# Transformer block pair in fp32 on one core: where the memory squares, the first low parts and the first down panels' high parts stand in the queues of a feed-forward stage

## The chip, the cores and the metric

One Trainium2 chip, one core of it. The metric is the device time of one execution in microseconds (us); of several runs the median is given. Engines are named as in the profile: PE is TensorE, DVE VectorE, ACT ScalarE, POOL GpSimd, SP SyncE, which issues the weight loads.

## What is computed

A sequence of 512 tokens of width 1024 goes through two blocks. The first is a feed-forward (2816 wide), a mixer, an attention over 256 memory tokens and a second feed-forward; the second block is a mixer of three branches and a third feed-forward. What matters here is cut to this:

```python
def swiglu(h, w1, w3, w2):
    return (jax.nn.silu(h @ w1) * (h @ w3)) @ w2

def first_block(x, mem, ...):
    x = x + 0.5 * swiglu(rms_norm(x, norm_ffn1[l]), ffn1_w1[l], ffn1_w3[l], ffn1_w2[l])
...
    x = x + memory_attention(rms_norm(x, norm_mem_q[l]), rms_norm(mem, norm_mem_kv[l]), ...)
    x = x + 0.5 * swiglu(rms_norm(x, norm_ffn2[l]), ffn2_w1[l], ffn2_w3[l], ffn2_w2[l])

def second_block(x, mem, ...):
...
    x = x + rmsnorm((jax.nn.silu(gate) * up) @ w_ffn_down[l], g_post_ffn[l])
```

All inputs are float32. `rms_norm(mem)` needs the mean square of the memory over its 1024 features, 8 tiles of 128.

## The kernel before

All activations lie feature-first in SBUF: `x` is 8 tiles of 128 features by 512 tokens, `hid` 22 tiles for the hidden layer, `memh` 8 tiles by 256 memory tokens. Each float32 product is made of three fp32r products: a high part of both operands, high by low and low by high. ACT copies a weight panel to its high part (`parts[..][0]`, semaphore `highs`), POOL subtracts to get the low part (`splits`), and PE may then use the panel. For activations ACT makes the high part (`hhis`) and DVE the low part (`hlos`).

**A feed-forward stage** runs three times (`ffn`, `ffn_up`, `ffn_down` on each engine). It begins with eight whole panels (two of them before the norm is known), whose products make the hidden tiles 0 to 3. Then come 9 pairs of hidden tiles (`PAIRS` = 8 turns of a loop and a last turn written out), each pair done by a seven-product scheme of blocks with sums and differences of quarter panels. PE runs `pair(0)`, `pair(1)` in each turn, 14 quarter products of 12 matmuls; the last turn has 12 quarter products. DVE makes three sums of weights for each half turn (`weight_sum_1`, `_2`, `_4`, in PSUM banks 3 and 7), the low parts of these sums (`sum_low`, `vlows`), and the gate and hidden tiles (`gate_first`, `up_second`, `gate_second`, `gate_scaled`, `pair_hidden`). ACT makes the high parts (`step_high`), copies partial outputs (`second_sum`, `third_taken`, `seed`) and does the silu (`pair_silu`). POOL makes four low parts (`first_lows`) and a difference for each half turn. Each engine goes through its own list in order, and the lists meet in semaphores; in a loop their values are computed from the turn.

**The down projection** takes 32 panels of 4 or 7 k-tiles (`CHUNKS`), eight banks at a time. Its first chunk uses the hidden tiles 0 to 3, whose high and low parts lie in `stores[0]` (tensor `bigr`). On ACT `high_part` makes a panel's high part; it waits for the panel's load and for the product that frees the parts.

In the first and second feed-forward DVE also sums the squares of the memory: `memory_square(k)` is a multiply into `sc` and an add into `ssum`, each waiting for the one before (`msteps`). PE turns the sum into column sums by `memory_norm` (L915), ahead of the first down panel, and waits there for `msums`. The third feed-forward has no memory squares (`loads` is None).

Where that work stands before: square 0 ahead of the pairs; squares 1 to 4 at the end of turns 0 to 3, square 5 behind turn 3 and 6 behind turn 7, between two loops; square 7 behind the last turn, in front of `memory_norm`. `EARLY` cuts the 8 turns in two loops of 4, and behind each loop two tiles of high parts (ACT, L2428) and low parts (DVE, `low_part`, L3182) of the first chunk are made. ACT makes the high parts of the down panels 0 and 1 behind the last `pair_silu` (L2457, L2458).

## Time and profile before

| | us |
|---|---|
| median of 3 runs | 2347.22 (2346.03 to 2347.31) |
| profiled execution, its own time | 2360.01 |
| span from first to last instruction | 2358.2 |
| PE busy in the span | 2262.5 (96%) |
| DVE, ACT, POOL busy | 1108.2, 1070.6, 1153.8 (47%, 45%, 49%) |

The mean granted clock of PE is 0.983 of full speed. A timeline row gives start, length, engine, line, what it writes and reads, and in brackets how long the engine was idle before it and what ended that. Matmul lengths overlap; starts are what to subtract.

### The profile page before, as it was taken

The page shows a single profiled execution, that of the slowest core. Times are in us where ns is not written, and L with a number is a line of the kernel's source. Part 1 is how long each engine was busy: PE and PEld are TensorE (multiplying, and loading weights), DVE is VectorE, ACT ScalarE, POOL GpSimd, SP SyncE. Part 2 cuts the span into 40 slices and gives each one's busy share as a digit, 9 for nine tenths or more (in the row PEclk, how much of TensorE's full clock was granted, in tenths as well). Part 3 has the DMA queues.
Part 4 walks back from the last instruction along what each step waited for, and adds up shares of the span by engine and source line. Part 5 has one row for each costly group of instructions (what it writes and reads, how often), then busy time and mean ns, then how long its engine had stood idle before and what let it go on. Part 6 is the DMA issues. An engine that isn't in the chain of part 4 may idle for free. (4 is left out here: it accounts for less than half of the span.)

```text
span 2358.2 us, 35280 instructions
## 1 busy us (share of the span) xinstructions
PE 2262.5 (96%) x12536; PEld 1903.8 (81%) x12536; DVE 1108.2 (47%) x2070; ACT 1070.6 (45%) x2037; POOL 1153.8 (49%) x723
## 2 busy tenths in 40 slices
PE   7999899999999999998999999999999998999997
PEld 6999688777787789997877777677788877899886
DVE  5777423323342337776143588735511123677511
ACT  5455333334554544554233366635522234555433
POOL 3666447842362446664444532043344443576545
PEclk9999999999999999999999999999999999999998
DMA  4323233422221222232353211022132322223232
GB/s 172 103 90 107 67 94 126 143 76 69 70 90 57 69 91 102 94 107 75 99 149 84 72 54 37 19 72 63 41 94 89 101 94 63 94 103 106 80 97 93
DMA packets 81275, 206.59 MB, mean 88 GB/s; under 512 B 7440, under 2 KB 31120, under 8 KB 80912
## 3 DMA queue, kind: packets, MB, share of 16 engines
q1 hardware_dynamic: 72832, 191.92, 25.4%
q10 hardware_dynamic: 8336, 13.25, 2.0%
q8 instruction: 67, 1.10, 0.2%
q14 instruction: 40, 0.33, 0.0%
HBM read 199.71 MB, written 2.10 MB: 86 GB/s over the span
## 5 line engine op out<-in xcount | busy, mean ns | idle before, releaser
L667 POOL TENSOR_TENSOR parts<-slot,parts 128x512 fp32r<-128x512 f32 (+3 forms) x210 | 383.6, 1828 | 305.4 <-ACT parts L2255 303.7
L692 POOL TENSOR_TENSOR parts<-slot,parts 128x512 fp32r<-128x512 f32 x162 | 222.4, 1383 | 200.3 <-ACT parts L2307 196.7
L2255 ACT ACTIVATE parts<-slot 128x1024 fp32r<-128x1024 f32 (+2 forms) x173 | 156.8, 909 | 335.4 <-PE bank L901 289.5
L896 PE MATMUL bank<-hhi,parts 128*128 128x512 f32 x576 | 227.1, 394 | 6.3 <-POOL parts L667 3.6
L897 PE MATMUL bank<-hhi,parts 128*128 128x512 f32 x576 | 225.9, 392 | 0.0
L655 POOL TENSOR_TENSOR parts<-slot,lanes 128x1024 fp32r<-128x1024 f32 x42 | 81.1, 1932 | 245.4 <-PE bank L1796 116.2
L1058 PE MATMUL bank<-hhi,parts 128*128 128x256 f32 x756 | 192.1, 286 | 2.4 <-ACT sc L2351 2.0
L1059 PE MATMUL bank<-hhi,parts 128*128 128x256 f32 x756 | 191.5, 285 | 0.0
L664 POOL TENSOR_TENSOR parts<-slot,parts 128x512 fp32r<-128x512 f32 x55 | 71.3, 1297 | 220.6 <-ACT parts L2255 219.0
L1058 PEld LDWEIGHTS bank<-hhi,parts 128*128 128x128 f32 x756 | 146.3, 194 | 4.7 <-issue 4.6
L1059 PEld LDWEIGHTS bank<-hhi,parts 128*128 128x128 f32 x756 | 146.3, 194 | 0.1
L901 PE MATMUL bank<-hlo,parts 128*128 128x512 f32 x576 | 144.8, 391 | 0.0
L2307 ACT ACTIVATE parts<-bank 128x512 fp32r<-128x512 f32 x159 | 91.0, 597 | 104.9 <-DVE bank L3242 85.4
L896 PEld LDWEIGHTS bank<-hhi,parts 128*128 128x128 f32 x576 | 109.2, 190 | 32.1 <-issue 6.4
L2307 ACT ACTIVATE parts<-slot 128x512 fp32r<-128x512 f32 x162 | 100.0, 627 | 62.4 <-PE bank L1061 39.0
L897 PEld LDWEIGHTS bank<-hhi,parts 128*128 128x128 f32 x576 | 109.2, 190 | 22.8 <-issue 0.2
L901 PEld LDWEIGHTS bank<-hlo,parts 128*128 128x128 f32 x576 | 108.2, 188 | 22.3
L1061 PE MATMUL bank<-hlo,parts 128*128 128x256 f32 x756 | 122.1, 284 | 0.0
L3255 DVE TENSOR_TENSOR parts<-bank,parts 128x512 fp32r<-128x512 f32 x159 | 104.5, 684 | 17.4 <-ACT parts L2307 17.4
L1061 PEld LDWEIGHTS bank<-hlo,parts 128*128 128x128 f32 x756 | 105.2, 193 | 0.0
L841 POOL TENSOR_TENSOR parts<-slot,parts 128x1024 fp32r<-128x1024 f32 x24 | 60.0, 2498 | 79.1 <-ACT parts L3064 78.8
L3967 DVE TENSOR_TENSOR ex<-silu,bank 128x512 f32<-128x512 f32 x24 | 16.5, 688 | 172.5 <-PE bank L2177 172.5
(679 smaller groups left out, 5965.5 us busy)
## 6 DMA issues: line engine op xcount, KB each, us to landing
slot<-w SPq DMA_DIRECT2D x264, 512.0 KB, 3.6
slot<-w SPq DMA_DIRECT2D x88, 256.0 KB, 2.7
slot<-w SPq DMA_DIRECT2D x48, 448.0 KB, 3.2
hid<-w SPq DMA_DIRECT2D x8, 512.0 KB, 3.5
x<-xT ACTq DMA_DIRECT2D x4, 512.0 KB, 9.7
hid<-headtab ACTq DMA_DIRECT2D x8, 256.0 KB, 3.7
big<-cmpw ACTq DMA_DIRECT2D x4, 512.0 KB, 10.8
hid<-w SPq DMA_DIRECT2D x8, 256.0 KB, 2.5
```

What stands on the lines that cost most here:

```text
L655: pool.tensor_tensor(high, w, nought.unsqueeze(2).to_broadcast([P, KD, P]), ALU.add).then_inc(highs, 1)
L667: pool.tensor_tensor(low, w, high.bitcast(F32), ALU.subtract).then_inc(splits, 1)
L692: pool.tensor_tensor(low, source, high.bitcast(F32), ALU.subtract).then_inc(splits, 1)
L896: pe.matmul(out, high[:, k, :], mhi[:, k, :], start=(start and k == 0), stop=False)
L897: pe.matmul(out, low[:, k, :], mhi[:, k, :], start=False, stop=False)
L901: mm = pe.matmul(out, high[:, k, :], mlo[:, k, :], start=False, stop=(stop and k == kt - 1))
L1058: pe.matmul(out, high[:, k, :], high_of(k), start=(start and k == 0), stop=False, skip_group_check=True)
L1059: pe.matmul(out, low[:, k, :], high_of(k), start=False, stop=False, skip_group_check=True)
L1061: mm = pe.matmul(out, high[:, k, :], low_of(k), start=False, stop=(stop and k == HK - 1), skip_group_check=True)
L2255: act.activation(parts[nth % 2][:, 0, 0:kt, :], slot[j][:, 0:kt, :], ACT.Copy).then_inc(highs, 1)
L2307: act.activation(w_flat(w_parts[s][0]), source, ACT.Copy).then_inc(highs, 1)
L3255: dve.tensor_tensor(low, bank[b][:, :], high.bitcast(F32), ALU.subtract).then_inc(vlows, 1)
```

## The change

Four things are moved; no arithmetic is added or taken away.

1. The memory squares stand inside the pair turns, one in each of the 8 turns, between the third `sum_low` and `gate_second(0)`. The wait of `memory_norm` is on the constant count of all steps.
2. The high and low parts of the hidden tiles 0 to 3 for the first down chunk stand inside turns 0 to 3: on ACT behind `third_taken(0)`, on DVE behind the `sum_low` that ends the weight work of the turn, ahead of `gate_second(1)`.
3. On the way in, DVE makes the first weight sum's low part and the second weight sum ahead of the last whole panel's gate and hidden tile, ACT makes the high part of STEP 1 ahead of that silu, and POOL makes the low part of it without waiting for the later ones.
4. ACT makes the high parts of down panels 0 and 1 ahead of the last `pair_silu(1)`, and SP loads slots 0 and 1 for them one POOL split earlier.

```diff
-EARLY = ((4, (0, 1)), (4, (2, 3)))
+EARLY = (4, 4)
...
                         if events is FFN_DOWN and j < RING:
                             if j == 2:
                                 sp.wait_ge(vsums, n.at("vsums"))
-                            else:
-                                sp.wait_ge(splits, n.at("splits", -2 if j < 2 else 0))
+                            sp.wait_ge(splits, n.at("splits", (-3, -3, -2, 0)[j]))
...
-            def first_lows(u, last=False, later=0):
+            def first_lows(u, last=False, later=0, ahead=0):
...
-                quarter_low(made + k + 2, used[k + 1], w1[:, HK:KD, :])
+                quarter_low(made + k + 2 - ahead, used[k + 1], w1[:, HK:KD, :])
...
             def memory_norm():
-                pe.wait_ge(msums, n.at("msums", 1))
+                pe.wait_ge(msteps, (1 + 2 * KD) * n.at("msums", 1))
...
+            def early_high(k):
+
+                act.activation(tile(stores[0][0], k), tile(hid, k), ACT.Copy).then_inc(hhis, 1)
...
                 third_taken(0, 4 + 3)
+                if early is not None:
+                    early_high(early)
                 step_high(7, last)
...
                 third_taken(1, 4 + 10)
-                if not last:
+                if last:
+                    high_part(0, 0, 4 + 7, load=2, kt=CHUNKS[0])
+                    high_part(1, 1, 4 + 11, load=2, kt=CHUNKS[0])
+                else:
...
                 quarter_high(0, -1, w_flat(slot[0][:, 0:HK, :]))
+                quarter_high(STEP_SLOT[1], -1, w_flat(slot[0][:, HK:KD, :]))
...
-                for k in range(5):
+                for k in (0, 2, 3, 4):
                     step_high(k)
...
-                high_part(0, 0, -5, kt=CHUNKS[0])
-                high_part(1, 1, 0, kt=CHUNKS[0])
...
+            def early_low(k):
+
+                dve.wait_ge(hhis, n.at("hhis", 1))
+                dve.tensor_tensor(tile(stores[0][1], k), tile(hid, k), tile(stores[0][0], k).bitcast(F32),
+                                  ALU.subtract).then_inc(hlos, 1)
...
                 sum_low(STEP_SLOT[7], 2 + 8, sum_bank[1][1])
+                if squared is not None:
+                    memory_square(squared)
                 gate_second(0, 4 + 7)
...
                     sum_low(STEP_SLOT[0], 2 + 15, sum_bank[0][1])
+                    if early is not None:
+                        early_low(early)
                     gate_second(1, 4 + 14)
...
-                if loads:
-                    memory_square(0).then_inc(msteps, 1)
-                    n.past({"msteps": 2})
+                sum_low(4, 5, sum_bank[0][0])
+                weight_sum_2(0, ahead=1)
                 raw_gate(1, 4, 3)
                 token_low(2)
-                sum_low(4, 5, sum_bank[0][0])
                 raw_hidden(1, 5, 3, 4, 2)
                 n.past(SECOND)
-                weight_sum_2(0)
+                sum_low(STEP_SLOT[0], 4, sum_bank[0][1])
                 token_low(3)
-                sum_low(STEP_SLOT[0], 3, sum_bank[0][1])
...
-                        if first:
-                            memory_square(i + 1).then_inc(msteps, 1)
-                    done += turns
-                    if loads:
-                        memory_square(4 + done // 4).then_inc(msteps, 1)
-                        n.past({"msteps": 2})
-                    for k in early:
-                        low_part(0, k)
+                        pair_turn(i * 2 + (4 + 2 * done), squared=i + done if loads else None, early=None if nth else i)
...
                 pair_turn(4 + 2 * done, True)
-                if loads:
-                    memory_square(KD - 1).then_inc(msums, 1)
-                    n.past({"msteps": 2})
```

How the queues read now, at the three places that matter. DVE, the end of a turn of the first loop, before (L3290 is the last hidden tile, L3187 and L3189 the square, L3182 the two low parts behind the loop):

```order
L3287 TENSOR_TENSOR silu<-bank,rinv 128x512 [waits gates_activated]
L3289 ISA [waits bank6_free]
L3289 TENSOR_TENSOR hid<-silu,bank 128x256
L3290 TENSOR_TENSOR hid<-hid,silu 128x256
L3186 REGISTER_ALU
L3187 ISA [waits memory_square_steps]
L3187 TENSOR_TENSOR sc<-memh 128x256
L3189 TENSOR_TENSOR ssum<-ssum,sc 128x256 [waits memory_square_steps]
...
L3182 TENSOR_TENSOR bigr<-hid,bigr 128x512 [waits h_high_parts] x2
```

and with the change, in the middle of the turn (L3281 is `up_second`, L3266 `sum_low`, L3192 and L3194 the square, L3287 `gate_second`; L3199, the early low part, stands in the second half of the turn):

```order
L3281 TENSOR_TENSOR hid<-bank,sc 128x256
L3265 REGISTER_ALU
L3266 TENSOR_TENSOR parts<-bank,parts 128x512 [waits panel_high_parts]
L3191 REGISTER_ALU
L3192 ISA [waits memory_square_steps]
L3192 TENSOR_TENSOR sc<-memh 128x256
L3193 REGISTER_ALU
L3194 TENSOR_TENSOR ssum<-ssum,sc 128x256 [waits memory_square_steps]
L3286 REGISTER_ALU
L3287 TENSOR_TENSOR bank<-bank,sc 128x256 [waits panel_products]
...
L3199 TENSOR_TENSOR bigr<-hid,bigr 128x512
```

The square left the end of the turn for the place in front of the second gate half.

DVE on the way into the pairs, before (L3220 and L3228 are the last whole panel's gate and hidden tile, L3255 `sum_low`, L3242 the second weight sum):

```order
L3187 TENSOR_TENSOR sc<-memh 128x256 [waits memory_square_steps]
L3189 TENSOR_TENSOR ssum<-ssum,sc 128x256 [waits memory_square_steps]
L3220 TENSOR_TENSOR ex<-bank,rinv 128x512 [waits panel_products]
...
L3228 TENSOR_TENSOR hid<-silu,bank 128x512 [waits panel_products,gates_scaled_by_the_norm]
L3242 TENSOR_TENSOR bank<-bank,slot 128x512 [waits low_parts_of_weight_sums,slot0_loaded]
L3215 TENSOR_TENSOR hlo<-hid,hhi 128x4x256 [waits token_sums_high_parts]
L3255 TENSOR_TENSOR parts<-bank,parts 128x512 [waits panel_high_parts]
```

and with the change (L3253 is the second weight sum, L3239 the hidden tile, L3266 `sum_low`):

```order
L3266 TENSOR_TENSOR ex_r<-bank,var_r 128x512 [waits panel_high_parts]
L3253 TENSOR_TENSOR bank<-bank,slot 128x512 [waits low_parts_of_weight_sums,slot0_loaded]
L3231 TENSOR_TENSOR ex<-bank,rinv 128x512 [waits panel_products]
...
L3239 TENSOR_TENSOR hid<-silu,bank 128x512 [waits panel_products,gates_scaled_by_the_norm]
L3266 TENSOR_TENSOR parts<-bank,parts 128x512 [waits panel_high_parts]
L3226 TENSOR_TENSOR hlo<-hid,hhi 128x4x256 [waits token_sums_high_parts]
```

The second weight sum passed the gate and the hidden tile, and the low part that PE waits for passed the fourth token sum's low part.

ACT at the end of the last turn, before (L2351 is `third_taken(1)`, L2356 `pair_silu(1)`, L2255 `high_part`):

```order
L2351 ACTIVATE sc<-bank 128x256 [waits panel_products]
L2356 ACTIVATE bank<-ex 128x512 [waits gates_before_silu_complete]
L2255 ACTIVATE parts<-slot 128x512 [waits panel_products,slot0_loaded]
L2255 ACTIVATE parts<-slot 128x512 [waits panel_products,slot1_loaded]
L2255 ACTIVATE parts<-slot 128x512 [waits panel_products,slot2_loaded]
```

and with the change:

```order
L2353 ACTIVATE sc<-bank 128x256 [waits panel_products]
L2257 ACTIVATE parts<-slot 128x512 [waits panel_products,slot0_loaded]
L2257 ACTIVATE parts<-slot 128x512 [waits panel_products,slot1_loaded]
L2358 ACTIVATE bank<-ex 128x512 [waits gates_before_silu_complete]
L2257 ACTIVATE parts<-slot 128x512 [waits panel_products,slot2_loaded]
```

Two panels passed the silu.

## Rows read from the trace of the kernel before

**Rows 1.** Waits of PE in the whole run: us in total, times, longest
```profile
PE bank L915 <- DVE ssum L3189: 11.3, 2, 5.7
PE bank L1058 <- DVE parts L3255: 10.5, 9, 2.3
```
**Rows 2.** Windows over the three pair stretches: start:end, length, busy by engine, PEclk, DMA
```profile
62.29:255.02 192.73, 185.71 (x1513) 183.33 (x1511) 143.60 (x249) 101.84 (x201) 122.12 (x88) 0.98 0.28 95
888.38:1080.62 192.24, 185.63 (x1513) 183.25 (x1511) 142.46 (x249) 101.83 (x201) 122.35 (x88) 0.98 0.28 96
2032.75:2216.82 184.07, 181.41 (x1513) 179.93 (x1511) 134.18 (x234) 101.23 (x200) 121.69 (x88) 1.00 0.30 100
```
**Rows 3.** Timeline of PE: first pair product behind the way in, first and third stage
```profile
67.54 0.38 PE L1058 MATMUL bank<-qs_r,parts 128*128 128x256 f32 x1 [1.87 <-DVE parts L3255]
2036.39 0.38 PE L1058 MATMUL bank<-qs_r,parts 128*128 128x256 f32 x1 [0.63 <-DVE parts L3255]
```
**Rows 4.** Timeline of PE: products behind the ends of turns, first and third stage
```profile
117.18 0.38 PE L1058 MATMUL bank<-PT_r,parts 128*128 128x256 f32 x1 [0.38 <-DVE parts L3255]
160.61 0.38 PE L1058 MATMUL bank<-PT_r,parts 128*128 128x256 f32 x1 [2.28 <-DVE parts L3255]
2124.74 0.38 PE L1058 MATMUL bank<-PT_r,parts 128*128 128x256 f32 x1 [0.57 <-DVE parts L3255]
2205.33 0.36 PE L1058 MATMUL bank<-PT_r,parts 128*128 128x256 f32 x1 [0.31 <-issue]
```
**Rows 5.** Windows: behind the wait at 67.54, and one steady turn
```profile
69.20:72.20 3.00, 3.00 (x16) 3.00 (x15) 0.16 (x1) 1.03 (x3) 3.00 (x3) 0.50 0.00 0
2094.00:2114.00 20.00, 20.00 (x171) 20.00 (x170) 14.48 (x25) 10.75 (x22) 13.85 (x10) 1.00 0.33 111
```
**Rows 6.** Timeline of DVE: a square at a turn's end, the next turn's start, an idle place
```profile
93.25 1.52 DVE L3187 TENSOR_TENSOR sc<-memh 128x256 f32 x1
95.21 0.42 DVE L3261 TENSOR_TENSOR ex<-bank,rinv 128x256 f32<-128x256 f32 x1
...
2107.11 0.43 DVE L3276 TENSOR_TENSOR bank<-bank,sc 128x256 f32<-128x256 f32 x1 [2.29 <-PE bank L1061]
```
**Rows 7.** Timeline of DVE: the first early low part behind turn 3, third stage
```profile
2121.29 1.79 DVE L3182 TENSOR_TENSOR bigr<-hid,bigr 128x512 fp32r<-128x512 f32 x1
```
**Rows 8.** Timeline of PE: from the last pair product into the down panels, first stage
```profile
254.38 0.64 PE L1061 MATMUL bank<-hlo,parts 128*128 128x256 f32 x4
260.67 1.22 PE L915 MATMUL bank<-ssum,consts 128*128 128x256 f32 x2 [5.65 <-DVE ssum L3189]
...
266.81 0.40 PE L896 MATMUL bank<-bigr,parts 128*128 128x512 f32 x1
269.59 0.39 PE L896 MATMUL bank<-bigr,parts 128*128 128x512 f32 x1
272.31 0.39 PE L896 MATMUL bank<-bigr,parts 128*128 128x512 f32 x1
...
279.24 0.47 PE L896 MATMUL bank<-bigr,parts 128*128 128x512 f32 x1 [4.05 <-POOL parts L667]
283.45 0.59 PE L896 MATMUL bank<-bigr,parts 128*128 128x512 f32 x1
```
**Rows 9.** The same, starts of panel 1 of the second stage, panels 0 and 1 of the third
```profile
1091.06 0.39 PE L896 MATMUL bank<-bigr,parts 128*128 128x512 f32 x1
2220.38 0.77 PE L896 MATMUL bank<-bigr,parts 128*128 128x512 f32 x1 [3.56 <-issue]
2225.64 0.59 PE L896 MATMUL bank<-bigr,parts 128*128 128x512 f32 x1
```
**Rows 10.** Timeline of POOL and of DVE: splits beside low parts, first stage
```profile
273.28 7.06 POOL L667 TENSOR_TENSOR parts<-slot,parts 128x512 fp32r<-128x512 f32 x2 [1.39 <-ACT parts L2255]
...
273.68 4.30 DVE L3182 TENSOR_TENSOR hlo<-hid,hhi 128x512 fp32r<-128x512 f32 x7
```
**Rows 11.** Timeline of ACT: the last silu, first stage
```profile
255.98 0.60 ACT L2356 ACTIVATE bank<-ex 128x512 f32<-128x512 f32 x1 [4.33 <-DVE ex L3281]
```

More of the change, by code:

```diff
@@ L2423, in ffn_up @@
                 step_high(5)
-                for turns, early in EARLY:
-                    with n.turns(act, turns, PAIR_TURN):
-                        pair_turn()
-                    for k in early:
-                        act.activation(stores[0][0][:, k, :], hid[:, k, :], ACT.Copy).then_inc(hhis, 1)
+                for nth, turns in enumerate(EARLY):
+                    with n.turns(act, turns, PAIR_TURN) as i:
+                        pair_turn(early=None if nth else i)
                 pair_turn(True)
@@ L3356, in ffn_up @@
                 done = 0
[L3357 to L3368 removed]
+                for nth, turns in enumerate(EARLY):
+                    events = {**PAIR_TURN, **(dict(msteps=2) if loads else {}), **({} if nth else dict(hhis=1, hlos=1))}
+                    with n.turns(dve, turns, events) as i:
+                        pair_turn(i * 2 + (4 + 2 * done), squared=i + done if loads else None, early=None if nth else i)
+                    done += turns
+                n.past({"hhis": -EARLY[0], "hlos": -EARLY[0]})
+                if loads:
+                    n.past({"msteps": 1})
                 pair_turn(4 + 2 * done, True)
[L3370 to L3372 removed]
                 n.past(PAIR_REST)
```

21 lines of the change are left out of this document (8 added, 13 removed).

## The prediction

> **What bounds the kernel now.** I began with the page's busy shares: PE is busy 96% of the span, so only what PE idles, or runs at the lower clock, can be won. Then the waits of PE, longest first. Two groups belong to work that the change moves: 11.3 us in 2 waits on the last memory square, and 10.5 us in 9 waits on low parts of weight sums [rows 1]. A wait does not say what it costs in all, since the clock falls behind it. So I read windows over the pair stretches of the three feed-forward stages, from the first quarter product to the end of the last. They hold the same 1513 matmul records; the first two, with memory squares, take 192.73 and 192.24 us, the third, without, 184.07 [rows 2]. A steady turn takes 20.00 us at full clock with PE never idle [rows 5]. Last I read the timelines at the way in, the turns' ends and the way out.
>
> **Way in and turns.** In the first stage PE waits 1.87 us for the low part of the second weight sum [rows 3], and the 3.00 us behind it run at a granted clock of 0.50, that is 1.2 instead of 2.4 GHz, though PE is never idle in them [rows 5]: half of 3.00, 1.5 us more. The third stage, without square 0, waits 0.63 [rows 3]. The new order takes square 0 away and puts the second weight sum ahead of a gate and a hidden tile. What is then late next is ACT's chain of seed, high part and low part behind the first quarter product; I leave 0.1 us of wait for it.
>
> A square at a turn's end keeps DVE from 93.25 to 95.21, 1.96 us [rows 6]. Behind such a delay the product in the next turn's sixth place waits only 0.38 us; behind turn 3, where two squares and two low parts stand together, 2.28. In the third stage the two low parts alone open 0.57 and, behind the loop, 0.31 [rows 4]. So a turn's end forgives about 1.6 us (1.96 less 0.38) and the rest is paid, with the clock's share on top.
>
> In its new place the square starts when DVE has ended the third weight sum's low part and would idle 2.29 us for PE [rows 6]. The square's 1.96 us (already with the multiply stretched to 1.52 beside POOL) fits in, by 0.3. Lower bound of its cost 0; upper bound: as if it stood at the end, 1.96 per turn, less the 1.6 forgiven. I take 0, the row of the place itself. The early low part took 1.79 us where POOL was busy [rows 7], and goes to the same idle place of the half turn behind; nearest row again 2.29, so 0, and if it is late by 0.5, the 1.6 cover it. ACT's early high part (0.6 us) stands in front of a high part that waits for DVE, 0 as well. POOL is busy 13.85 of a turn's 20.00 us [rows 5]; a few tenths of blocking per turn are covered. The register instructions that the moved lines bring with them are not counted as busy, and I give them nothing.
>
> All three stretches should then take what the third takes, less 0.57, 0.31 and 0.53: 182.66. Gain: 192.73 + 192.24 + 184.07 - 3 x 182.66 = **21.1 us**. If squares kept their whole price only 1.4 would be left.
>
> **Way out.** First stage: the last pair product ends at 255.02 (254.38 + 0.64); PE waits 5.65 us for square 7, and from 260.67 the two column sums and panel 0 take 6.14 us, where a panel at full clock takes 2.72 (269.59 to 272.31); panel 1 starts at 266.81 [rows 8]. That is 11.79 us from the last product to panel 1. With the change nothing is left to wait for: the squares end in the last looped turn, the low parts of tiles 0 to 3 in turn 3, and the two high parts, which so far follow the last silu at 255.98, are made in the 4.33 us in which ACT idled before it [rows 11] (half a panel's copy is about as long as that silu, 0.60); the second one waits for the last product but one, so both POOL splits are done around 255. SP's first two loads leave one split earlier, at a time at which SP has no other to issue. PE keeps its clock: 0.1 to start, 0.4 for the column sums (6.14 us at the lower clock is 3.1 at the higher, 2.72 of it the panel), and 2.72 make 3.2. Gain 8.6. Second stage: from 1080.62 [rows 2] to 1091.06 [rows 9], 10.44, less 3.2: 7.2. Third stage, with no column sums: idle 3.56 and panel 1 at 2225.64 [rows 9], 8.82 from 2216.82, less 2.8: 6.0. Sum **21.8 us**. ACT's table load and root for the memory norm stay between panels 0 and 1, where they stood relative to PE; DVE's reciprocal (after the last hidden tile) comes about 0.2 us before ACT asks for it. That is the work late next, and it costs at most tenths.
>
> **Sum.** 21.1 + 21.8 = 42.9. The profiled execution took 2360.01 and would take 2317.1; it stands 12.8 over the median, and I take the same difference from the median: 2347.22 - 42.9 = **2304.3 us**. A measurement of this kernel tells about 0.2% (4.7 us) from no change.
>
> **A stall that may come or go (rivals 1 and 2).** In the first stage panel 4 starts at 279.24 after 4.05 us of idleness and takes 4.21 us (to 283.45) instead of 2.72 [rows 8]: from 272.31 it is 6.93 to the start, 4.2 over 2.72, and 1.5 for the clock, 5.7 in all. POOL's split for it started at 273.28 and, with the next one's 1.3, lasted 7.06, while DVE ran seven low parts in 4.30 us without a gap [rows 10]. The second stage runs the same lists and shows no such wait. So it hangs on tens of nanoseconds. The change lets both stages begin the down panels at full clock, as the second stage nearly did; that speaks for the stall to go: 2304.3 - 5.7 = 2298.6 (rival 1). It could also appear in both: 2310.0 (rival 2). The likeliest case leaves the count as it is, or the timed runs never had it.
>
> The Trainium skill (SBUF — State Buffer, Who interferes with whom) says that a DVE instruction with two SBUF inputs and a GpSimd instruction that reads SBUF take the shared ports one at a time, and that who starts first holds them for its whole instruction. By that rule a split would be kept waiting by one low part of 0.68 us and not by seven: the stall would not be there at all, and the trace disagrees here with 4.3 us, and where the rule did hold after the change the time would be rival 1's. The rule speaks against the change as well, since squares and early low parts now stand beside POOL's four splits of a half turn; by it each costs POOL one instruction at most.
>
> **Rival 3, the moved work does not fit.** For: the square has only 0.3 us to spare, and DVE's idle time varies from turn to turn. Against: 1.6 us forgiven behind it. If the first two stretches stay as they are, 2304.3 + 10.1 + 9.6 = 2324.0; half of it, 2314.
>
> **Rival 4, the last part does not do what it says.** The first down panels wait still, for a load, a bank or the hidden tile, until about where the third stage starts now: 3.56 idle and 2.5 of clock in each stage, 2304.3 + 18 = 2322.
>
> **Rival 5, slower.** Place: beside POOL's splits in the turns. Price: a square or early low part keeps POOL out as the low parts did, 4.3 us [rows 10]; less the 1.6 that is forgiven, with 1.5 for the clock behind it, 4.2 us each. There are 16 + 12 such places. It decides from 11 of them on (42.9 / 4.2); all of them give 2304.3 + 118 = 2422. Against: here DVE has one or two such instructions in a row, not seven, and squares at turns' ends met a busy POOL and were themselves the ones delayed (1.52).
>
> **Chances.** Forecast 0.46, rival 1 0.28, rival 2 0.08, rival 3 0.08, rival 4 0.05, rival 5 0.05. Only a small part of rivals 3 to 5 lies within 0.2% (0.01); slower 0.04; faster 0.95. Range: from 2294 (rival 1 and the bounds of some tenths in each place) to 2318 (rival 2, half of rival 3); what is left out is under 2 in 10. The forecast's own range is 2300 to 2309.
>
> **What would show it.** PE's waits on L915's source are gone; the three pair stretches are within 1 us of each other near 182.7 us with a clock of 1.00; DVE idles a few tenths, no longer 2.29, before `gate_second(0)`; panel 0 takes 2.7 us in each stage. It is wrong if PE waits in turns on low parts or splits, if a first panel waits over 1 us, or if the pair stretches keep 190.

## The result, and the profile after

| | before | after |
|---|---|---|
| median of 4 runs each, us | 2346.62 (2345.39 to 2347.31) | 2305.41 (2304.71 to 2306.63) |
| ratio | | 0.9825 (0.9808 to 0.9843) |
| profiled execution, its own time / span | 2360.01 / 2358.2 | 2304.71 / 2302.9 |
| mean granted clock of PE | 0.983 | 0.991 |
| PE, DVE, ACT, POOL busy | 2262.5, 1108.2, 1070.6, 1153.8 | 2240.7, 1116.5, 1072.3, 1160.6 |

The change makes the kernel 41 us faster; the forecast was 2304.3. Measured again later beside other kernels it stood at 2304.42, with before at 2350.26: ratio 0.9812 (0.9794 to 0.9829). The span of the profile fell by more, 55.3 us. One later execution of the kernel before took 6613.34 us, far from all others, and is left out of every comparison.

The lines move by two or so: the pair products are L1060, L1061 and L1063 now, the panels L898, L899 and L903, the column sums L917, `sum_low` L3266, the square L3192 and L3194, the early low part L3199, `gate_second` L3287, `high_part` L2257, `third_taken` L2353, the splits L669.

The same three windows as in [rows 2], from the first quarter product to the end of the last (start:end, length, busy of PE, PEld, DVE, ACT, POOL, granted clock, DMA share, GB/s):

```profile
62.48:243.72 181.24, 180.18 (x1514) 179.80 (x1513) 145.13 (x250) 103.10 (x201) 127.44 (x90) 1.00 0.30 102
862.88:1044.08 181.20, 180.18 (x1514) 179.80 (x1513) 148.65 (x250) 101.91 (x201) 127.06 (x89) 1.00 0.31 102
1987.21:2168.41 181.20, 180.18 (x1514) 179.80 (x1513) 137.70 (x234) 102.55 (x201) 125.56 (x90) 1.00 0.30 102
```

All three take the same time now, at full clock, and shorter than the third did before. Of the two groups of waits in [rows 1] one is gone: L917, the column sums, has no wait. The other is the second row here (us in total, times, longest), 1.0 us where it was 10.5. The first row is none of the two and was there before as well, with 2.0 us in 3 waits:

```profile
PE bank L1060 <- ACT sc L2353: 2.1, 3, 0.7
...
PE bank L1060 <- DVE parts L3266: 1.0, 3, 0.3
```

One wait of 0.35 us on the way in and the untouched one of 0.7 in the last turn are all that is left in a pair stretch. The way out of the first stage, on PE's timeline, answers to [rows 8]:

```profile
241.64 0.64 PE L1063 MATMUL bank<-hlo,parts 128*128 128x256 f32 x4
242.12 0.28 PE L1060 MATMUL bank<-hhi,parts 128*128 128x256 f32 x1
...
243.08 0.64 PE L1063 MATMUL bank<-hlo,parts 128*128 128x256 f32 x4
243.56 0.59 PE L917 MATMUL bank<-ssum,consts 128*128 128x256 f32 x2
243.80 0.58 PE L898 MATMUL bank<-bigr,parts 128*128 128x512 f32 x1
...
246.75 0.39 PE L898 MATMUL bank<-bigr,parts 128*128 128x512 f32 x1
...
249.47 0.39 PE L898 MATMUL bank<-bigr,parts 128*128 128x512 f32 x1
...
252.19 0.39 PE L898 MATMUL bank<-bigr,parts 128*128 128x512 f32 x1
...
254.91 0.39 PE L898 MATMUL bank<-bigr,parts 128*128 128x512 f32 x1
```

Column sums and panel 0 follow the last product (its end is 243.72) without a gap, panel 1 starts 3.03 us after that end instead of 11.79, and panels 1, 2 and 3 take 2.72 each: the stall before panel 4 of [rows 8] is not there. The reason stands on ACT's and POOL's timelines. ACT:

```profile
240.22 0.62 ACT L2257 ACTIVATE parts<-slot 128x512 fp32r<-128x512 f32 x1
242.38 0.63 ACT L2257 ACTIVATE parts<-slot 128x512 fp32r<-128x512 f32 x1 [1.54 <-PE bank L1063]
244.68 0.60 ACT L2358 ACTIVATE bank<-ex 128x512 f32<-128x512 f32 x1 [1.67 <-DVE ex L3292]
```

The two high parts fill what was idle ahead of the last silu [rows 11]; the first split runs on POOL from 240.92 to 242.21, the second from 243.09 to 244.37. And on DVE's timeline the second half of a turn of the first loop, with its early low part, and the first half of the next turn, with its square:

```profile
103.74 0.68 DVE L3199 TENSOR_TENSOR bigr<-hid,bigr  x1
106.03 0.43 DVE L3287 TENSOR_TENSOR bank<-bank,sc 128x256 f32<-128x256 f32 x1 [1.62 <-PE bank L1063]
...
113.67 0.41 DVE L3192 TENSOR_TENSOR sc<-memh 128x256 f32 x1
114.12 1.40 DVE L3194 TENSOR_TENSOR ssum<-ssum,sc 128x256 f32<-128x256 f32 x1
115.99 0.43 DVE L3287 TENSOR_TENSOR bank<-bank,sc 128x256 f32<-128x256 f32 x1 [0.47 <-PE bank L1063]
```

Where DVE idled 2.29 us [rows 6] the square leaves 0.47 of it, the low part 1.62. Here `gate_second` still waits for PE and not PE for it. Not every turn has that room: behind three of the second stage's eight squares, and behind four of the eight early low parts of the second and third stages (1.79 us long there), `gate_second` follows without idle time, once 0.6 us late (at 976.83, 10.56 us behind the one before it instead of 10.0). PE waits in none of these turns either. It is the add that is stretched beside POOL now (1.40), not the multiply.

Where the span's 55.3 us went, by starts of rows in the two traces:

| | before | after | gained | forecast |
|---|---|---|---|---|
| pair stretch, stage 1 | 192.73 | 181.24 | 11.5 | 10.1 |
| stage 2 | 192.24 | 181.20 | 11.0 | 9.6 |
| stage 3 | 184.07 | 181.20 | 2.9 | 1.4 |
| last product to panel 1, stage 1 | 11.79 | 3.03 | 8.8 | 8.6 |
| stage 2 | 10.44 | 3.03 | 7.4 | 7.2 |
| stage 3 | 8.82 | 2.59 | 6.2 | 6.0 |
| stall before panel 4, stage 1 | 5.7 | 0 | 5.7 | 0 |

That is 47.8 without the stall and 53.5 with it; the other 1.8 us lie in parts of the kernel that no edit touched. The timed runs gained 41 in the first comparison and 46 in the second.

### The profile page after: what moved, and what is told of

It reads as the page before. It is cut to its first block and busy times, and to the rows that moved or that the text cites. A ratio compares the mean times of both kernels' runs of the same rounds, so it can differ in the third digit from the quotient of the medians.

```text
span 2302.9 us, 35359 instructions
## 1 busy us (share of the span) xinstructions
PE 2240.7 (97%) x12536; PEld 1889.8 (82%) x12536; DVE 1116.5 (48%) x2070; ACT 1072.3 (47%) x2037; POOL 1160.6 (50%) x723
## 5 line engine op out<-in xcount | busy, mean ns | idle before, releaser
L669 POOL TENSOR_TENSOR parts<-slot,parts 128x512 fp32r<-128x512 f32 (+3 forms) x210 | 379.6, 1808 | 284.1 <-ACT parts L2257 282.4
L694 POOL TENSOR_TENSOR parts<-slot,parts 128x512 fp32r<-128x512 f32 x162 | 229.2, 1428 | 164.3 <-ACT parts L2309 161.7
L2257 ACT ACTIVATE parts<-slot 128x1024 fp32r<-128x1024 f32 (+2 forms) x173 | 157.2, 910 | 312.1 <-PE bank L903 262.5
L898 PE MATMUL bank<-hhi,parts 128*128 128x512 f32 x576 | 226.4, 393 | 5.8 <-ACT hhi L2266 2.7
L899 PE MATMUL bank<-hhi,parts 128*128 128x512 f32 x576 | 225.0, 391 | 0.0
L1060 PE MATMUL bank<-hhi,parts 128*128 128x256 f32 x756 | 188.7, 282 | 2.1 <-ACT sc L2353 2.1
L1061 PE MATMUL bank<-hhi,parts 128*128 128x256 f32 x756 | 189.0, 282 | 0.0
L666 POOL TENSOR_TENSOR parts<-slot,parts 128x512 fp32r<-128x512 f32 x55 | 71.3, 1297 | 220.7 <-ACT parts L2257 219.1
L1060 PEld LDWEIGHTS bank<-hhi,parts 128*128 128x128 f32 x756 | 144.1, 191 | 2.7 <-issue 2.6
L903 PE MATMUL bank<-hlo,parts 128*128 128x512 f32 x576 | 144.6, 390 | 0.0
L1061 PEld LDWEIGHTS bank<-hhi,parts 128*128 128x128 f32 x756 | 144.2, 191 | 0.1
L898 PEld LDWEIGHTS bank<-hhi,parts 128*128 128x128 f32 x576 | 108.7, 189 | 31.6 <-DVE ex L3231 4.1
L899 PEld LDWEIGHTS bank<-hhi,parts 128*128 128x128 f32 x576 | 108.7, 189 | 22.6 <-issue 0.2
L903 PEld LDWEIGHTS bank<-hlo,parts 128*128 128x128 f32 x576 | 108.0, 188 | 22.3
L1063 PE MATMUL bank<-hlo,parts 128*128 128x256 f32 x756 | 121.3, 283 | 0.0
L3266 DVE TENSOR_TENSOR parts<-bank,parts 128x512 fp32r<-128x512 f32 x159 | 104.6, 684 | 18.5 <-ACT parts L2309 18.5
L1063 PEld LDWEIGHTS bank<-hlo,parts 128*128 128x128 f32 x756 | 104.2, 192 | 0.0
```

The source lines that it names most:

```text
L669: pool.tensor_tensor(low, w, high.bitcast(F32), ALU.subtract).then_inc(splits, 1)
L694: pool.tensor_tensor(low, source, high.bitcast(F32), ALU.subtract).then_inc(splits, 1)
L898: pe.matmul(out, high[:, k, :], mhi[:, k, :], start=(start and k == 0), stop=False)
L899: pe.matmul(out, low[:, k, :], mhi[:, k, :], start=False, stop=False)
L903: mm = pe.matmul(out, high[:, k, :], mlo[:, k, :], start=False, stop=(stop and k == kt - 1))
L1060: pe.matmul(out, high[:, k, :], high_of(k), start=(start and k == 0), stop=False, skip_group_check=True)
```

## The experiments

All but the ones named so start from the changed kernel. Two windows are compared in each trace: the pair stretch (181.2 is the changed kernel's) and the time from its end to panel 0 and through it (0.08 and 2.95 in the first stages, where 2.95 holds the rest of the column sums). Losses are given against the changed kernel's second median, 2304.42, which was not taken beside all of these runs; so a loss is exact to a few us only. The kernel before stood at 2349.11 beside "squares back", "panels behind silu" and "early low parts", at 2350.26 beside "after again", "old way in" and the repeated multiplies, and at 2349.55 beside the last four.

| run | median us | ratio to before |
|---|---|---|
| after again | 2304.42 (2300.18 to 2309.27) | 0.9812 (0.9794 to 0.9829) |
| before again | 2353.51, one run | |
| squares back | 2327.70 (2324.35 to 2332.00) | 0.9902 (0.9888 to 0.9915) |
| panels behind silu | 2323.45 (2316.16 to 2337.74) | 0.9901 (0.9874 to 0.9928) |
| early low parts behind loops | 2310.73 (2308.11 to 2314.75) | 0.9837 (0.9822 to 0.9851) |
| old way in | 2308.34 (2301.41 to 2308.83) | 0.9812 (0.9794 to 0.9830) |
| multiply twice | 2315.59 (2315.04 to 2316.71) | 0.9856 (0.9841 to 0.9871) |
| multiply four times | 2348.55 (2343.40 to 2352.64) | 0.9991 (0.9981 to 1.0000) |
| squares at turns' ends | 2318.65 (2314.52 to 2322.30) | 0.9864 (0.9841 to 0.9887) |
| multiply behind the last turn | 2316.18 (2314.36 to 2316.88) | 0.9858 (0.9836 to 0.9879) |
| panels behind silu, low parts spaced | 2319.47 (2315.66 to 2323.81) | 0.9868 (0.9845 to 0.9890) |
| before, low parts spaced | 2350.15 (2344.58 to 2353.39) | 1.0000 (0.9987 to 1.0013) |

### Each part undone by itself

**Squares back**: part 1 is undone, the other three stay.

```diff
+                if loads:
+                    memory_square(0)
+                    n.past({"msteps": 2})
...
-                        pair_turn(i * 2 + (4 + 2 * done), squared=i + done if loads else None, early=None if nth else i)
+                        pair_turn(i * 2 + (4 + 2 * done), early=None if nth else i)
+                        if first:
+                            memory_square(i + 1)
                     done += turns
+                    if loads:
+                        memory_square(4 + done // 4)
+                        n.past({"msteps": 2})
...
                 pair_turn(4 + 2 * done, True)
+                if loads:
+                    memory_square(KD - 1)
+                    n.past({"msteps": 3})
```

> The changed kernel with the eight memory squares back in their old places (one ahead of the pairs, four at the ends of turns, one behind each loop, one in front of the column sums); the other three parts of the change stay. Theory (squares at the ends of turns and in front of the column sums are paid on TensorE, the clock's fall behind them too): pair stretches of the first two stages 8 to 10 us longer than 181.2, way out 8 us longer in each, together 32 to 36: near 2339. Rival (the clock's share is a matter of the one profiled execution): only the waits, 4 + 5.7 per stage: near 2325. Rival (the squares were hidden and the first down panels' high parts were the bound): under 5 us.

It lost 23.3 against the changed kernel: 5.5 and 6.0 in the two stretches (186.73, 187.18), and behind them 5.8 and 6.9. The third stage, without squares, is unchanged at 181.20. So the squares were what made the first two stages longer, but for less than I had set; the time is near the rival's 2325. One reason is in the pair stretches. With the other parts of the change in place PE waits 0.56 and 0.32 on the way in of the first stage instead of 1.87, and 1.44 behind turn 3 instead of 2.28, and the clock granted over the stretch is 1.00 instead of 0.98. Another is on the way out. PE waits there for square 7, from its timeline:

```profile
254.47 1.11 PE L917 MATMUL bank<-ssum,consts 128*128 128x256 f32 x2 [3.93 <-DVE ssum L3194]
```

3.93 where it was 5.65 [rows 8]. DVE's timelines tell why; in the kernel before

```profile
257.68 1.07 DVE L3290 TENSOR_TENSOR hid<-hid,silu 128x256 f32<-128x256 f32 x1
258.67 1.48 DVE L3187 TENSOR_TENSOR sc<-memh 128x256 f32<-128x256 f32 x1
260.19 0.42 DVE L3189 TENSOR_TENSOR ssum<-ssum,sc 128x256 f32<-128x256 f32 x1
```

and here

```profile
253.21 0.42 DVE L3301 TENSOR_TENSOR hid<-hid,silu 128x256 f32<-128x256 f32 x1
253.54 0.42 DVE L3192 TENSOR_TENSOR sc<-memh 128x256 f32<-128x256 f32 x1
253.99 0.42 DVE L3194 TENSOR_TENSOR ssum<-ssum,sc 128x256 f32<-128x256 f32 x1
```

Before, the last hidden tile and the multiply each ran beside the two splits of panels 0 and 1, which POOL made from 257.20 to 259.87; with part 4 in place it has ended them at 251.19. Part 4 had thus already given back 1.7 us of the square's wait, a crossing of two parts that my sum did not have.

**Panels behind silu**: part 4 is undone.

```diff
-                            sp.wait_ge(splits, n.at("splits", (-3, -3, -2, 0)[j]))
+                            else:
+                                sp.wait_ge(splits, n.at("splits", -2 if j < 2 else 0))
...
-                if last:
-                    high_part(0, 0, 4 + 7, load=2, kt=CHUNKS[0])
-                    high_part(1, 1, 4 + 11, load=2, kt=CHUNKS[0])
-                else:
+                if not last:
...
+                high_part(0, 0, -5, kt=CHUNKS[0])
+                high_part(1, 1, 0, kt=CHUNKS[0])
```

> The changed kernel with the high parts of down panels 0 and 1 behind the last silu again, and the old loads. Theory: in each of the three stages the first panel waits 3.6 us and runs at the lower clock for 2.5 more: 3 x 6 = 18, near 2323. Rival (a first panel was bound by the last hidden tile anyway): no difference, 2305. The clock's share alone in doubt: 3 x 3.6 = 11, 2316.

It lost 19.0. The stretches stay at 181.20, 181.20 and 181.20; panel 0 starts 3.55, 3.56 and 3.56 us after the last product and takes 5.25, 5.26 and 4.41. With a few tenths in panel 1 that is 17.6 us, in all three stages: with the squares gone from the way out, the splits would have held panel 0 nearly as long. The stall came back too, once, in the first stage of the profiled execution. PE:

```profile
248.38 0.76 PE L899 MATMUL bank<-bigr,parts 128*128 128x512 f32 x1 [3.12 <-issue]
...
266.11 0.77 PE L899 MATMUL bank<-bigr,parts 128*128 128x512 f32 x1 [3.72 <-POOL parts L670]
```

**Early low parts behind loops**: part 2 is undone, high parts and low parts of tiles 0 to 3 go behind turns 3 and 7, two each.

```diff
-                        pair_turn(early=None if nth else i)
+                        pair_turn()
+                    for k in (2 * nth, 2 * nth + 1):
+                        act.activation(stores[0][0][:, k, :], hid[:, k, :], ACT.Copy).then_inc(hhis, 1)
...
+                    for k in (2 * nth, 2 * nth + 1):
+                        low_part(0, k)
```

> The changed kernel with the high and low parts of hidden tiles 0 to 3 between the loops again, two and two. Theory: the waits of the third stage before, 0.57 + 0.31, in each of the three stages, 2.6 us: 2308. Rival (early low parts beside POOL's splits cost inside the turns): faster than 2305.4.

The stretches grew by 1.7, 1.7 and 2.0 (182.94, 182.92, 183.18), in all 5.4, and the median by 6.3: more than expected. PE's timeline of the first stage shows where the rest is:

```profile
153.60 0.63 PE L1063 MATMUL bank<-hlo,var_r 128*128 128x256 f32 x4
154.57 0.38 PE L1060 MATMUL bank<-PT_r,parts 128*128 128x256 f32 x1 [0.34 <-DVE parts L3268]
...
156.24 0.35 PE L1060 MATMUL bank<-hhi,parts 128*128 128x256 f32 x1
```

Without a wait the product after a group of four starts 0.48 us after the group's start (241.64 to 242.12 above); here it starts 0.97 after it. The row shows a wait of 0.34, so 0.15 more is lost before it, in the end of the group that the next product no longer overlaps. Behind it the product takes 1.67 to the next one, where one without a wait takes 1.44 (242.12 to 243.56): 0.23 more. **A wait shown as 0.34 costs 0.72**, at full clock. Over all waits of this run the excess is larger, some 0.5 each: 5.4 us were lost for 2.2 of shown waits in six places.

**Old way in**: part 3 is undone.

```diff
-                sum_low(4, 5, sum_bank[0][0])
-                weight_sum_2(0, ahead=1)
                 raw_gate(1, 4, 3)
                 token_low(2)
+                sum_low(4, 5, sum_bank[0][0])
...
+                weight_sum_2(0)
+                token_low(3)
+                sum_low(STEP_SLOT[0], 3, sum_bank[0][1])
...
-                for k in (0, 2, 3, 4):
+                for k in range(5):
```

> The changed kernel with the old order on the way into the pairs (gate and hidden tile ahead of the second weight sum, the fourth token sum's low part ahead of STEP 0's), without square 0, which stays in the turns. Theory: each stage then has the way in of the third stage before, a wait of 0.63 or a little more instead of 0.35: 1 to 3 us in all, 2308. Rival (the new order is what took away the 1.87 us wait and the clock's fall behind it): 3 x 3 = 9 and more, 2315.

The stretches took 181.55, 181.41 and 182.60, so 0.35, 0.21 and 1.4 more, with waits of 0.70, 0.56 and 1.09 in place of 0.35. The medians, 2308.34 and 2304.42, cannot tell 2 us apart (five runs of each spread over 7 and 9, and both ratios are 0.9812). On the way in of the first two stages either repair does most of the work: of the 1.87 us [rows 3] 0.70 are left with the square gone and the old order, and 0.88 (0.56 and 0.32) with the square back and the new order. Only the third stage, which has no square, needs the reordering. There a second wait is back too, 0.39 for ACT's `second_sum`, which the third stage had before:

```profile
2049.81 0.39 PE L1058 MATMUL bank<-o_sb_r,var_r 128*128 128x256 f32 x1 [0.35 <-ACT sc L2346]
```

### Where a square is free

**Multiply twice** and **multiply four times**: the multiply of each square is repeated, each one waiting for the one before, in the place of the changed kernel.

```diff
                 dve.tensor_tensor(sc[:, 0, 0:M], tile(memh, k), tile(memh, k), ALU.mult).then_inc(msteps, 1)
                 dve.wait_ge(msteps, n.at("msteps", 2))
+                dve.tensor_tensor(sc[:, 0, 0:M], tile(memh, k), tile(memh, k), ALU.mult).then_inc(msteps, 1)
+                dve.wait_ge(msteps, n.at("msteps", 3))
```

> The changed kernel with each memory square's multiply done twice in place (the same product into the same tile, a wait between), so that DVE is busy 0.5 to 1.5 us longer in each of the 16 turns that hold a square. Theory of the prediction (2.29 us of idleness take 1.96, and another 1.6 are forgiven): at most 2 us, 2306. Rival (the place is full, each tenth over it is paid): 16 x 0.5 to 1.0 = 8 to 16, 2313 to 2321.

> The same with three more multiplies, 1.5 to 3.5 us more on DVE in each of 16 turns, 3.5 to 5.5 in all. Theory: past 2.29 + 1.6 = 3.9 us it is paid: 0 to 1.6 us and some 0.3 of restart per turn, 5 to 30 us, 2310 to 2335, with waits of PE on weight sums' low parts in each turn. If it still costs nothing, the slack was read too small by half.

With one multiply more the first two stretches took 187.59 and 187.51, 12.7 more in all, and the third was untouched. DVE in the third turn, and PE's waits in that turn and in the next:

```profile
116.59 0.42 DVE L3192 TENSOR_TENSOR sc<-memh 128x256 f32 x1
117.04 1.40 DVE L3194 TENSOR_TENSOR sc<-memh 128x256 f32 x1
118.48 1.41 DVE L3196 TENSOR_TENSOR ssum<-ssum,sc 128x256 f32<-128x256 f32 x1
119.81 0.42 DVE L3289 TENSOR_TENSOR bank<-bank,sc 128x256 f32<-128x256 f32 x1
```

```profile
124.30 0.39 PE L1060 MATMUL bank<-hhi,parts 128*128 128x256 f32 x1 [0.97 <-ACT sc L2353]
...
145.51 0.39 PE L1060 MATMUL bank<-hhi,parts 128*128 128x256 f32 x1 [0.97 <-ACT sc L2353]
```

The extra multiply costs 1.44 (beside POOL) in a place with 0.47 to spare; `gate_second` is then about 1 us late. ACT's silu and high parts wait for DVE's next instructions, and ACT's `third_taken` (L2353) behind them lets PE wait 0.97, not once but in the turns that follow too. My text let a turn's end forgive 1.6 us. These runs show that this allowance is one for the stage and not one for each turn: the first two turns take the delay without a wait of PE, and from the third turn on every turn pays. Six waits a stage of 0.44 to 0.98 us stand in the trace, 8.6 us in all with both stages, for 12.7 us lost: 0.34 each over what is shown. Four multiplies made 201.64 and 201.61 of the stretches, 40.8 more, and ate the whole gain of the change (ratio 0.9991). The page shows 30.5 us of waits for it, of which 28.4 in the 14 places inside turns; there the waits reach 2.8 us and the rest is 0.9 each. Part of that rest is the lower clock: behind three of the seven waits of the first stage (2.55, 2.73 and 2.25 us) the clock granted over the next 5.5 to 6.2 us was 0.69 to 0.76, behind the other four (1.45 to 1.52, and another of 2.25) it was 1.00.

**Squares at turns' ends**: all eight squares leave the place before `gate_second` for the end of their turns. All else is as changed, square 0 not ahead of the pairs and square 7 not behind them.

```diff
-                if squared is not None:
-                    memory_square(squared)
                 gate_second(0, 4 + 7)
...
+                        if loads:
+                            memory_square(i + done)
```

> The changed kernel with the eight squares at the ends of the eight turns, none behind the last turn. Same work in the same turns, another place. Theory (the idle place in front of the second gate half is what hides them): each turn's end waits 0.2 to 0.4 and pays 0.3 of restart, 8 x 0.6 = 5 per stage, 2314. Rival (a delay of 1.96 is forgiven at a turn's end, so only the square behind the last turn and the double ones cost): under 2 us, 2306.

The stretches took 188.61 and 188.54, 14.7 more in all. The same 16 squares cost nothing in front of `gate_second` and about 0.9 us each here. DVE at the end of a turn, and PE behind it:

```profile
112.67 1.52 DVE L3192 TENSOR_TENSOR sc<-memh 128x256 f32 x1
114.23 0.43 DVE L3194 TENSOR_TENSOR ssum<-ssum,sc 128x256 f32<-128x256 f32 x1
114.62 0.42 DVE L3272 TENSOR_TENSOR ex<-bank,rinv 128x256 f32<-128x256 f32 x1
114.97 1.28 DVE L3266 TENSOR_TENSOR parts<-bank,parts 128x512 fp32r<-128x512 f32 x2
```

```profile
115.78 0.38 PE L1060 MATMUL bank<-PT_r,parts 128*128 128x256 f32 x1 [0.28 <-DVE parts L3266]
```

The low part of the next weight sum stands behind the square in DVE's list, and PE needs it in the sixth place of the turn. Fifteen such waits, 6.7 us in all, stand for the 14.7 lost, again some 0.5 each over what is shown. It is the place and not the number or the length of the squares that part 1 gains by. The rival, that a turn's end forgives them, is out.

**Multiply behind the last turn**: a ninth multiply, whose result is not used, stands where square 7 stood, and the column sums wait for it.

```diff
-                pe.wait_ge(msteps, (1 + 2 * KD) * n.at("msums", 1))
+                pe.wait_ge(msteps, (2 + 2 * KD) * n.at("msums", 1))
...
                 pair_turn(4 + 2 * done, True)
+                if loads:
+                    dve.tensor_tensor(sc[:, 0, 0:M], tile(memh, 0), tile(memh, 0), ALU.mult).then_inc(msteps, 1)
+                    n.past({"msteps": 1})
```

> The changed kernel with one more multiply of a memory tile behind the last turn of the first two stages, for which the column sums wait as they did for square 7; the result of it is not used. Theory: PE waits 4 us in front of the column sums and runs the first panel at the lower clock, 5.5 to 6.5 in each of two stages: 11 to 13, near 2317. Rival (the first panel waits for the last hidden tile or a split anyway): under 2 us.

One instruction of 0.4 us, and the wait of the column sums for it, cost 11.8 us in the median (2316.18 against 2304.42). In the first stage PE waits, and starts the column sums at

```profile
247.11 1.22 PE L917 MATMUL bank<-ssum,consts 128*128 128x256 f32 x2 [3.47 <-DVE sc L3379]
```

and panel 0, which starts 4.12 us after the last product, takes 5.47 instead of 2.95: the clock granted is 0.50 from 247.11 on. In the second stage the wait is 3.47 again, panel 0 starts 3.81 after the last product and takes 4.53. What held PE there was DVE's whole tail of the stage (last gate, silu, hidden tile), of which the square was the last link.

### The stall before panel 4

**Panels behind silu, low parts spaced**, and **before, low parts spaced**: each of `low_part`'s instructions also waits for the one before it, so that DVE's chain is less dense.

```diff
                 dve.wait_ge(hhis, n.at("hhis", at + 1))
+                if k:
+                    dve.wait_ge(hlos, n.at("hlos", at))
```

> The kernel with part 4 undone (median 2323.5, but 2316.2 to 2337.7 in 6 runs, and in its profile a stall of 3.7 us in front of down panel 4 of the first stage, where POOL's split lasted through seven low parts of DVE), and in it each low part of the down chunks waits for the one before, so that DVE leaves the ports between two of them. Theory (the spread is this stall, it needs a chain of DVE instructions without a gap): no split over 2 us, runs within 4 us of each other, median 2316 to 2320. Rival (the spread is the clock or the chip): spread as before, over 10 us.

> The kernel before, with the same waits between low parts. Theory: its spread (2343.9 to 2354.4 beside this call's kernels) narrows to 5 us or less and the median falls by 0 to 5 us. Rival: the same spread and median.

In the trace of "panels behind silu", where the stall stands, POOL and DVE show the picture of [rows 10] again:

```profile
260.45 6.75 POOL L670 TENSOR_TENSOR parts<-slot,parts 128x512 fp32r<-128x512 f32 x2 [1.29 <-ACT parts L2258]
```

```profile
256.32 4.31 DVE L3171 SCALAR_TENSOR_TENSOR memh<-memh,params,rinv 128x256 f32<-128x256 f32 x8 [5.64 <-ACT rinv L2222]
260.55 4.29 DVE L3187 TENSOR_TENSOR hlo<-hid,hhi 128x512 fp32r<-128x512 f32 x7
```

and with the low parts spaced the same split, at the same place, is done in its own time:

```profile
260.61 1.35 POOL L670 TENSOR_TENSOR parts<-slot,parts 128x512 fp32r<-128x512 f32 x1 [1.27 <-ACT parts L2258]
```

```profile
260.74 7.18 DVE L3189 TENSOR_TENSOR hlo<-hid,hhi 128x512 fp32r<-128x512 f32 x5
```

DVE's low parts start 1.3 apart instead of 0.6, and nobody waits for that. Both traces with the stall have POOL's split start in the last one of the eight memory-norm instructions that run ahead of the seven low parts (260.45 against 260.55, 273.28 against 273.68). That line-up is not enough for a stall: in the second stage of "panels behind silu" the split starts at 1072.97 and the low parts at 1073.18, and the split took 1.45 us. So the one spaced split that got through in the same line-up (260.61 against 260.74) goes with the spacing, but does not show that the spacing did it. In the changed kernel DVE's same two chains stand at 249.41 and 254.68, and the split that falls into the low parts gets through in 1.83 us (255.88), while the seven take 6.49 instead of 4.30:

```profile
255.88 1.83 POOL L669 TENSOR_TENSOR parts<-slot,parts 128x512 fp32r<-128x512 f32 x1 [1.41 <-ACT parts L2257]
```

So either engine can be the one held. What decides between the two stays open. The Trainium skill (SBUF — State Buffer, Who interferes with whom) lets the engine that issues first keep the ports for one instruction. The last row agrees, with 0.5 us over the split's usual 1.3, and so does the spaced run; the two stalls, in which a split outwaited seven instructions, do not.

In the timed runs the spacing did little. "Panels behind silu" lost the two high ones of its six runs (2333.88 and 2337.74), and its range went from 21.6 to 8.2 us; the median moved by 4, with intervals that overlap. The kernel before kept its median (ratio 1.0000). With the spacing it spread over 8.8 us in 12 runs; without it, beside that one, 15 runs spread over 11.2 and one stood alone at 2360.24, the time of the profiled execution with the stall (2360.01). So, as far as times can tell, the stall is rare in the timed runs of before, and most of their spread is something else.

### The two kernels again

> The kernel before, unchanged, profiled once more. The profiled execution of it took 2360.0 us, 13 over its timed median, while the changed kernel's took 2304.7, as its timed runs do. If the 13 us belong to that one execution (the stall of 4.05 us in front of down panel 4 and the share of the lower clock come and go), the span is now near 2345 and some of these places are shorter: pair stretches below 192, no 4.05 us wait. If they belong to the kernel, the span is again near 2358 with the same waits.

> The changed kernel, unchanged, in the same call as the edits of it. Its times so far: 2304.7 to 2306.6, and its pair stretches are 181.2 us in all three stages with no wait for a split. If the spread of the kernel before (2346.7 to 2354.8 in 11 runs) comes from PE waits and a stall that comes and goes, this one stays within 3 us. If it comes from the chip, this one spreads by 8 as well.

Before's second trace has no stall (panels 1 to 3 take 2.73, 2.72 and 2.72 us and panel 4 follows), with stretches of 192.93, 191.24 and 184.46: the stall comes and goes in one and the same kernel. The changed kernel's stretches were 181.20, 181.19 and 181.46, but its runs spread over 9.1 us, the second of the two outcomes named, with pair stretches that hardly differ. The last section says where that sits.

## Why the prediction was right, point by point

- **Sum.** 42.9 was forecast; the timed runs gave 41.2 (interval 36.8 to 45.1) and in the second comparison 45.8 (40.2 to 48.4), the rows of the traces 47.8 without the stall. The two families of terms are real and hold it all. That 2304.3 was met to 1.1 us is partly luck: the terms were too small by 4.9, and the timed runs show 2 to 7 less than the rows do.
- **Pair stretches, 21.1 forecast, 25.4 measured.** The step that failed is the third stage's floor: "less 0.57, 0.31 and 0.53: 182.66". I took waits at their shown length, and left out a wait of 0.35 for ACT (2049.81, shown above). The third stage had 1.86 us of shown waits that the change bears on (0.63, 0.35, 0.57, 0.31); 0.35 of them is left, and the 1.5 removed were worth 2.9, since a wait costs 0.3 to 0.5 more than shown at full clock ("early low parts behind loops", "multiply twice"). All three stretches came out at 181.2.
- **Way in.** 0.1 us of wait was forecast, 0.35 is left; and the order of part 3 did less than I gave it in the first two stages, since with square 0 gone it gains only 0.35 and 0.21 there.
- **Squares at 0 in their new place.** Right in what they cost. The room was 0.23 us or more where 0.3 was forecast, except in three turns of the second stage, where none was left and a small reserve behind it did the rest. But the size of that reserve, "a turn's end forgives about 1.6 us", was wrong for a row of turns. One multiply more already cost 11 us. Rival 3 was nearer than its 0.08 said: it starts 0.5 us further on, with no reserve for each turn.
- **Early low parts at 0.** Right in what they cost; in four of the twelve turns no idle time was left, where they took 1.79 us as forecast.
- **Way out, 21.8 forecast, 22.4 measured.** Right in each stage within 0.2 us. Two of its causes overlap: late splits alone cost 17.6 us over three stages, one late multiply alone for 12 over two. Either repair by itself would have left much of the wait.
- **Rival 1** came true in the trace, not in the time: the stall is gone from the profile, and 5.7 of the 55.3 us of span are that. By their times the timed runs of before hardly ever had it, as the forecast's last clause allowed for. I had also said that the profiled execution would stay 12.8 over the median, and it stands at the median.
- **Rivals 4 and 5** are out: no first panel waits, and POOL was locked out nowhere in the turns, where its longest single split took 1.76 us.

Undone one by one, the parts are worth 23.3, 19.0, 6.3 and 2 to 4, together 51 to 53, while the whole is worth 41 to 46. The rows of the traces say where they cross. On the way out the parts give back 12.7 and 17.6, more than the 22.4 of the whole, since either fault alone brings back most of one and the same wait. In the pair stretches they give 11.5, 5.4 and 2.0, less than the whole's 25.4, since there two faults together open a longer wait, with the lower clock behind it, than each does alone (behind turn 3 of the first stage 2.28 against 1.44 and 0.34). The two crossings nearly cancel, 49.2 against 47.8; so most of the difference in the medians is likely the spread of some five runs each, taken beside different kernels; that was not tried.

## What to carry to other kernels

Work that nobody waits for soon costs nothing in front of a wait for PE that is longer than it, and about half its length or more anywhere else in a chain that is full; measure the idle time beside the neighbour that stretches it, and count on no reserve that must last for every turn. Behind the last product of a phase clear everything that the next phase's first product needs, even half a microsecond of it, for it hangs behind the whole tail of the slowest chain and brings the lower clock with it. Price a wait of PE at what the trace shows plus 0.3 to 0.5 us, and more once the clock falls.

## What I had not expected

**The spread of the runs sits in a part that no edit touched.** From the end of the second pair stretch to the start of the third (down projection, attention, second block, the same instructions) the changed kernel took 943.13 us in one profile and 939.03 in the other, and 948.62 with four multiplies, whose way out is the same. Windows over that part, then over the 120 matmul records behind one wait of 3.1 us in the attention, then from PE's wait for L1033 to the third pair stretch: after,

```profile
1044.08:1987.21 943.13, 914.06 (x4405) 723.41 (x4404) 412.82 (x854) 407.26 (x838) 378.10 (x214) 0.99 0.26 77
1268.09:1294.47 26.38, 26.38 (x120) 21.96 (x120) 16.69 (x44) 8.03 (x28) 15.34 (x10) 0.88 0.24 69
1931.77:1987.21 55.44, 53.97 (x260) 45.26 (x261) 32.80 (x43) 29.21 (x43) 19.56 (x9) 0.96 0.22 67
```

after again,

```profile
1045.39:1984.42 939.03, 909.76 (x4405) 720.65 (x4404) 414.96 (x854) 407.13 (x838) 379.72 (x214) 0.99 0.26 77
1269.80:1293.17 23.37, 23.36 (x120) 19.64 (x120) 17.58 (x44) 8.00 (x28) 16.35 (x10) 1.00 0.26 78
1928.93:1984.42 55.49, 54.03 (x260) 45.34 (x261) 33.69 (x43) 29.32 (x43) 19.43 (x9) 0.95 0.22 67
```

In the second window PE is busy throughout in both traces, behind the same wait (3.08 and 3.09 us); the clock granted was 0.88 in the one and 1.00 in the other, and the same matmuls took 3.0 us more. Behind a wait of 0.83 us, ending at 1492.68 (1491.35 in the other) 16 matmul records took 4.06 us at 0.58 and 2.37 at 1.00, another 1.7. These two places make 4.7 us; over the rest of the 939 to 943 us "after again" is the slower one, by 0.6. The third window is the same in both to 0.05 us; with four multiplies it took 58.58, at a clock of 0.89. The Trainium skill (TensorE: Matmul & The Clock Gate, Part 1: The HAM clock gate) says that the number of slow matmuls at the start of one kernel changes from run to run; here the same is seen in the middle of one. The change has not narrowed the spread: 9.1 us in five runs, with 10.5 in 15 of the kernel before beside them. What decides the clock in each execution was not tried.

**A wait of under 2 us can bring the lower clock.** In the kernel before, 1.87 us of wait [rows 3] were followed by a granted clock of 0.50 [rows 5], while a wait of 1.44 behind turn 3 in "squares back" was followed by 1.00, and the stretch with six waits of 0.47 to 0.98 us in "multiply twice" kept its clock:

```profile
63.99:251.58 187.59, 182.13 (x1514) 180.46 (x1513) 166.32 (x258) 100.19 (x201) 123.85 (x90) 1.00 0.29 98
```
